# 1/rms applied as products leave PSUM, from parts of the unnormed h, at the memory attention's norm and both PEER norms

## The chip, the cores and the metric

The kernel runs on one core of one Trainium2 chip. The metric is the device time of one launch, in microseconds (us). Shown are the median of three runs and one profiled execution; the profile gives the span from the first to the last instruction beside the time of that execution.

## The reference

Two transformer blocks over 256 tokens of width 1024, in float32. Each block is a mixer and a mixture of experts (PEER); the first has attention to a memory between them. Every part starts with an RMS norm of the residual h. Cut to what matters here:

```python
def rms_norm(x, g):
    y = x * lax.rsqrt(jnp.mean(x * x, axis=-1, keepdims=True) + EPS)
    return y * g

def first_block(...):
    h = h + concat([o_gla, o_nsa]) @ w_out
    h = h + cross_attn(rms_norm(h, norm_xattn), rms_norm(mem, norm_mem), xa_wq, xa_wk, xa_wv, xa_wo)
    h = h + peer_ffn(rms_norm(h, norm_ffn), peer_wq, peer_subkeys, peer_down, peer_up)

def second_block(...):
    h = h + hybrid_mixer(rmsnorm(h, norm_mix_g), ...)      # ends in "@ w_out"
    h = h + peer_ffn_2(rmsnorm(h, norm_ffn_g), peer_w_q, peer_subkeys, peer_u, peer_v)

def peer_ffn(hn, wq, subkeys, down, up):
    q = hn @ wq                       # queries: 8 heads x 2 halves
    s = einsum(q, subkeys)            # then top 16 of each half, top 16 of the pairs, softmax
    act = gelu(einsum(hn, down[experts])) * gate    # uses hn once more
    return einsum(act, up[experts])
```

## The kernel before

**Layout.** h is kept with channels on the 128 partitions: eight chunks (KD = 8) of 128 channels by 256 tokens. A weight unit is 128x1024 float32 (512 KB): all that is needed for 128 output channels. Products are made from two rounded parts of each operand, a high and a low one, as three fp32r matmuls (`product`, L367 to L372): 8 chunks x 3 = 24 matmuls for a unit.

**Weight units.** `Split` (L317) fetches one: SyncE loads it into one of three ring slots (L334), ScalarE writes the high part into one of three part buffers (L338), VectorE the low part (L343; in the PEER layers' down phase GpSimd does it, L349). The ring slot is free when the low part is made, the part buffer when TensorE has used it. `submit` keeps two fetched units ahead of the one being multiplied; `flush(a, b)` fetches the next matrix's first two units while it works off the last two.

**Order.** There is no scheduler: the program is a list of steps, and each engine runs its part of every step in the order of that list, with semaphore waits. An instruction that waits holds everything that comes after it on its engine.

**Around the three norms.** `to_h` multiplies the eight units of `w_out`, `xa_wo` or `w_out_2`. Behind each product VectorE adds it to h (`AddToH`, L511), GpSimd squares the new chunk of h (L527), and TensorE adds the squares over the partitions with a matmul of ones into bank 7 (`SumSquares`, L549), one unit late; the last of them comes after all products. Then comes a `Barrier` (L618: each of four engines drains and waits for the others). `Normalize` (L554) follows: VectorE makes mean + eps (L571), ScalarE the root (L587, with a table load), VectorE the reciprocal (L573), and then for each chunk VectorE h x gain x 1/rms (L577), ScalarE the high part (L592), VectorE the low part (L581). The first product of the next matrix waits for these parts, chunk by chunk.

The next matrix is `xa_wq` (eight units), `peer_wq` (eight) or `peer_w_q_2` (sixteen). Each product leaves PSUM by a ScalarE copy (`Keep`, L495). After the last one TensorE makes the scores: L1523 in the memory attention, L1645 in the first PEER layer, L1649 in the second. Both PEER layers load their subkeys (L293) ahead of the third query unit, after the barrier.

In the text a *site* is one of these places: X (memory attention), P1, P2 (PEER layers). F(i) is the fetch of the site's unit i, high and low part.

## Time and profile before

| what | value |
|---|---|
| median of 3 runs | 2694.74 us (2690.89 to 2695.68) |
| the profiled execution's own time | 2693.68 us |
| its span | 2691.6 us |
| TensorE matmul busy | 2463.5 us, 92% of the span |
| VectorE / ScalarE / GpSimd busy | 1770.1 (66%) / 1173.3 (44%) / 769.5 us (29%) |
| mean granted TensorE clock | 0.949 |
| HBM read over the span | 142 GB/s |

A matmul's busy time overlaps the next one's, since they are pipelined: inside a run of products one starts every 0.12 us and is shown with 0.28 us. A row of the timeline that begins before an earlier row has ended is such an overlap. Idle time ahead of an instruction stands in brackets with what ended it.

### The profile page before, as it was taken

How to read it: one execution, taken by the hardware profiler on the slowest of the kernel's cores; microseconds unless marked ns; L12 is line 12 of the kernel's file. 1: busy time of each engine (PE TensorE's matmuls, PEld its weight loads, DVE VectorE, ACT ScalarE, POOL GpSimd, SP SyncE). 2: the span in 40 equal slices, each digit the busy share in tenths (PEclk: the TensorE clock that was granted, in tenths of full speed). 3: DMA queues.
4: the chain of work that ended last, by engine and by line, in shares of the span. 5: the costliest groups of instructions: out<-in, count | busy, mean ns of one | idle time of the engine just before them, and what ended most of it. 6: DMA issues, size and time to landing. Idle time of an engine off the chain costs nothing.

```text
span 2691.6 us, 38806 instructions
## 1 busy us (share of the span) xinstructions
PE 2463.5 (92%) x15906; PEld 2221.8 (83%) x15906; DVE 1770.1 (66%) x2770; ACT 1173.3 (44%) x1962; POOL 769.5 (29%) x366
## 2 busy tenths in 40 slices
PE   6978888999999999997878888789999999999997
PEld 5876788999999788886757877579999999888885
DVE  4564447978888555556577275465987888555554
ACT  3354334444444444443443344234444444444442
POOL 3000103886666000001000053201886666100000
PEclk8887899999999999998888989889999999999998
DMA  5421335555544666663422343145555445566663
GB/s 166 126 86 56 90 91 165 164 167 148 146 145 150 181 189 187 189 188 119 126 84 87 123 126 113 52 141 158 164 165 150 148 149 144 175 188 188 188 188 103
DMA packets 108566, 384.37 MB, mean 143 GB/s; under 512 B 13007, under 2 KB 16000, under 8 KB 107816
## 3 DMA queue, kind: packets, MB, share of 16 engines
q1 hardware_dynamic: 108392, 381.91, 47.3%
q8 instruction: 127, 2.08, 0.3%
q14 instruction: 47, 0.39, 0.0%
HBM read 380.79 MB, written 1.06 MB: 142 GB/s over the span
## 4 chain that ended last, share of the span: by engine, by line
PE 78%; DVE 13%; ACT 4%; POOL 2%; issue 1%; DMA 1%; SPq 0%; DVEq 0%; POOLq 0%; ACTq 0%
PE psum L370 21%; PE psum L371 21%; PE psum L372 21%; PE psum L1805 4%; POOL weight_parts L349 2%; PE psum L402 2%; PE psum L549 1%; PE psum L2425 1%; PE psum L2195 1%; DVE weight_parts L343 1%; DVE peer_experts L1713 1%; PE psum L1271 1%; ACT weight_parts L338 1%; DVE peer_experts L1689 1%; DVE peer_experts L1681 1%
## 5 line engine op out<-in xcount | busy, mean ns | idle before, releaser
L370 PE MATMUL psum<-acts_high,weight_parts 128*128 128x256 f32 x3152 | 933.8, 296 | 72.1 <-DVE acts_low L581 28.4
L371 PE MATMUL psum<-acts_low,weight_parts 128*128 128x256 f32 x3152 | 904.7, 287 | 0.0
L372 PE MATMUL psum<-acts_high,weight_parts 128*128 128x256 f32 x3152 | 904.4, 287 | 0.0
L349 POOL TENSOR_TENSOR weight_parts<-weight_ring,weight_parts 128x1024 fp32r<-128x1024 f32 x276 | 697.6, 2536 | 649.9 <-ACT weight_parts L338 649.2
L338 ACT ACTIVATE weight_parts<-weight_ring 128x1024 fp32r<-128x1024 f32 x681 | 714.8, 1050 | 184.1 <-PE psum L372 96.7
L343 DVE TENSOR_TENSOR weight_parts<-weight_ring,weight_parts 128x1024 fp32r<-128x1024 f32 x405 | 497.7, 1231 | 363.8 <-ACT weight_parts L338 363.7
L370 PEld LDWEIGHTS psum<-acts_high,weight_parts 128*128 128x128 f32 x3152 | 617.2, 196 | 90.0 <-issue 42.7
L371 PEld LDWEIGHTS psum<-acts_low,weight_parts 128*128 128x128 f32 x3152 | 618.7, 196 | 2.6 <-issue 1.7
L372 PEld LDWEIGHTS psum<-acts_high,weight_parts 128*128 128x128 f32 x3152 | 617.4, 196 | 0.0
L370 PE MATMUL psum<-weight_parts,peer_coef 128*128 128x512 f32 x1024 | 405.2, 396 | 4.0 <-issue 3.9
L372 PE MATMUL psum<-weight_parts,peer_coef 128*128 128x512 f32 x1024 | 405.0, 396 | 0.0
L371 PE MATMUL psum<-weight_parts,peer_coef 128*128 128x512 f32 x1024 | 405.0, 395 | 0.0
L1876 ACT ACTIVATE peer_coef<-peer_experts 128x256 fp32r<-128x256 f32 x256 | 106.6, 417 | 362.4 <-PE psum L372 361.3
L1789 DVE TENSOR_TENSOR peer_onehots<-peer_onehots,peer_gates 128x512 f32<-128x512 f32 x128 | 248.1, 1938 | 4.4
L370 PEld LDWEIGHTS psum<-weight_parts,peer_coef 128*128 128x128 f32 x1024 | 192.4, 188 | 51.3 <-issue 4.2
L372 PEld LDWEIGHTS psum<-weight_parts,peer_coef 128*128 128x128 f32 x1024 | 192.4, 188 | 46.6
L371 PEld LDWEIGHTS psum<-weight_parts,peer_coef 128*128 128x128 f32 x1024 | 192.4, 188 | 46.2
L527 POOL TENSOR_TENSOR peer_experts<-h 128x256 f32<-128x256 f32 x16 | 9.7, 614 | 745.0 <-DVE h L511 744.9
L1880 DVE TENSOR_TENSOR peer_coef<-peer_experts,peer_coef 128x256 fp32r<-128x256 f32 x256 | 108.9, 426 | 159.5 <-ACT peer_coef L1876 159.5
L1786 DVE TENSOR_TENSOR peer_onehots<-psum,peer_pairs 128x1024 f32<-128x1024 f32 x128 | 155.1, 1212 | 0.1
L1853 ACT ACTIVATE psum<-psum 128x4 f32<-128x4 f32 (+25 forms) x156 | 41.4, 266 | 248.5 <-PE psum L372 248.5
L527 POOL TENSOR_TENSOR work<-h 128x256 f32<-128x256 f32 x40 | 29.8, 759 | 412.2 <-DVE h L511 395.4
(388 smaller groups left out, 2508.0 us busy)
## 6 DMA issues: line engine op xcount, KB each, us to landing
weight_ring<-in_peer_down SPq DMA_DIRECT2D x128, 512.0 KB, 3.6
weight_ring<-in_peer_up SPq DMA_DIRECT2D x128, 512.0 KB, 3.6
weight_ring<-in_peer_u SPq DMA_DIRECT2D x128, 512.0 KB, 3.6
weight_ring<-in_peer_v SPq DMA_DIRECT2D x128, 512.0 KB, 4.2
weight_ring<-in_w_in SPq DMA_DIRECT2D x88, 512.0 KB, 3.7
weight_ring<-in_w_out SPq DMA_DIRECT2D x16, 512.0 KB, 3.6
weight_ring<-in_peer_w_q SPq DMA_DIRECT2D x16, 512.0 KB, 4.2
weight_ring<-in_w_in_v SPq DMA_DIRECT2D x10, 512.0 KB, 4.1
```

What stands on the lines that cost most here:

```text
L338: q.e.activation(self.high, self.ring, ACT.Copy).then_inc(*self.rounded.once())
L343: q.e.tensor_tensor(self.low, self.ring, self.high.bitcast(F32), ALU.subtract).then_inc(*self.unit.ready.once())
L349: q.e.tensor_tensor(self.low, self.ring, self.high.bitcast(F32), ALU.subtract).then_inc(*self.unit.ready.once())
L370: q.e.matmul(out, sh, mh, start=first, stop=False)
L371: q.e.matmul(out, sh, ml, start=False, stop=False)
L372: return q.e.matmul(out, sl, mh, start=False, stop=last)
L402: last = q.e.matmul(self.out, w[:, k, :], acts.whole[:, k, :], start=k == 0, stop=k == KD - 1)
L1786: q.e.tensor_tensor(self.hot, over(over(self.c.bank(7)[:, 0:P], GROUP, 1), 2, 1), over(x.pairs[:, :, tokens], P, 3), ALU.is_equal).then_in ...
L1789: q.e.tensor_tensor(self.hot[:, 0, :, :], self.hot[:, 0, :, :], over(x.gates[:, tokens], P, 2), ALU.mult).then_inc(*self.ready.once())
L1805: last = q.e.matmul(out, self.hot[:, 0, t, :], self.hot[:, 1, t, :], start=True, stop=True)
L1876: q.e.activation(self.high, self.src, ACT.Copy).then_inc(*self.rounded.once())
L1880: q.e.tensor_tensor(self.low, self.src, self.high.bitcast(F32), ALU.subtract).then_inc(*self.ready.once())
```

## The change

`to_h` also makes, right behind each `AddToH`, the two parts of h x gain of that chunk, without 1/rms (`GainedActs`), in a second pair of buffers (`acts_spare`). The next matrix is multiplied from these, and 1/rms, which is one number for a token, is multiplied in as each product leaves PSUM (`Late`, on VectorE in place of the ScalarE copy). 1/rms itself (`Rstd`) is made beside the products; the last `SumSquares` stands behind the second product. The PEER layers need the normed h for their down phase, so there eight steps `NormalizeChunk` stand between the query products: two behind each of the products 2 to 5 at P1, one behind each of 2 to 9 at P2. The barriers at the three sites go, and the subkeys' load waits for the last product of `to_h` in their place. `xn_reversed` lives in the spare buffers now. The norms of both mixers, of the memory and the final ones stay.

```diff
@@ -410,6 +410,48 @@
 
     def pool(self, q):
         self.evac.pool(q, self.out, self.done)
+
+class LateChannels(Channels):
+    phases = 2
+    def tensor(self, q):
+        super().tensor(q)
+        yield
+    def scalar(self, q):
+        yield
+        self.evac.scalar(q, self.out, self.done)
+    def vector(self, q):
+        yield
+        self.evac.vector(q, self.out, self.done)
+
+def late_channels(c, srcs, acts, evac, make_norm, beside=()):
+    beside, waiting = list(beside), []
+    def make(unit, n):
+        step = c.plan(LateChannels(c, unit, acts, evac(n)))
+        waiting.append(step)
+        if n == 1:
+            beside.extend(make_norm())
+        if n >= 1:
+            while waiting:
+                c.plan(waiting.pop(0))
+        if n >= 2:
+            for _ in range(-(-len(beside) // max(1, len(srcs) - 2 - n))):
+                c.plan(beside.pop(0))
+    for n, src in enumerate(srcs):
+        c.submit(src, lambda unit, n=n: make(unit, n))
 
 
 class Tokens:
@@ -495,6 +537,22 @@
         q.e.activation(self.dst, out, self.func, bias=0.0, scale=self.scale).then_inc(*self.kept.once())
 
 
+
+class Late(Evac):
+    def __init__(self, dst, scale, c):
+        self.dst, self.scale, self.c = dst, scale, c
+    def out_of_psum(self, c):
+        self.scaled = c.last_kept = c.mark("late_scaled")
+        return self.scaled
+    def vector(self, q, out, done):
+        q.wait_ge(done)
+        q.e.scalar_tensor_tensor(out=self.dst, in0=out, scalar=self.scale, in1=self.c.rms, op0=ALU.mult,
+                                 op1=ALU.mult).then_inc(*self.scaled.once())
 class AddToH(Evac):
 
 
@@ -549,6 +607,66 @@
         last = q.e.matmul(self.out, self.ones, self.squares, start=self.k == 0, stop=self.k == KD - 1)
         if self.summed:
             last.then_inc(*self.summed.once())
+
+class Rstd(Step):
+    def __init__(self, c, tmp):
+        self.tmp, self.sums, self.summed = tmp, c.bank(7)[:, 0:T], c.summed
+        self.mean, self.root, self.ready = c.mark("mean_square"), c.mark("root"), c.mark("rstd")
+        c.bank_free[7] = (self.mean,)
+        c.rms = tmp
+    def vector(self, q):
+        q.wait_ge(self.summed)
+        q.e.tensor_scalar(self.tmp, self.sums, 1.0 / D, EPS, ALU.mult, ALU.add).then_inc(*self.mean.once())
+        q.wait_ge(self.root)
+        q.e.reciprocal(self.tmp, self.tmp).then_inc(*self.ready.once())
+        q.wait_ge(self.ready)
+    def scalar(self, q):
+        q.wait_ge(self.mean)
+        q.e.activation(self.tmp, self.tmp, ACT.Sqrt).then_inc(*self.root.once())
+
+class NormalizeChunk(Step):
+    def __init__(self, c, x, gain, out, tmp, parts, k):
+        self.x, self.gain, self.out, self.tmp = x[:, k, :], gain[:, k:k + 1], out[:, k, :], tmp
+        self.high, self.low, self.parts_free = parts.high[:, k, :], parts.low[:, k, :], parts.free
+        self.normed, self.rounded, self.ready = c.mark("normed"), c.mark("acts_high"), c.mark("acts_low")
+        parts.marks[k] = self.ready
+    def vector(self, q):
+        q.e.scalar_tensor_tensor(out=self.out, in0=self.x, scalar=self.gain, in1=self.tmp, op0=ALU.mult,
+                                 op1=ALU.mult).then_inc(*self.normed.once())
+        q.wait_ge(self.rounded)
+        q.e.tensor_tensor(self.low, self.out, self.high.bitcast(F32), ALU.subtract).then_inc(*self.ready.once())
+    def scalar(self, q):
+        q.wait_ge(self.parts_free, self.normed)
+        q.e.activation(self.high, self.out, ACT.Copy).then_inc(*self.rounded.once())
+
+class GainedActs(Step):
+    def __init__(self, c, x, gain, parts, k, after=()):
+        self.x, self.gain, self.high, self.low = x, gain[:, k:k + 1], parts.high[:, k, :], parts.low[:, k, :]
+        self.after, self.parts_free = tuple(after), parts.free
+        self.rounded, self.ready = c.mark("acts_high"), c.mark("acts_low")
+        parts.marks[k] = self.ready
+    def scalar(self, q):
+        q.wait_ge(self.parts_free, *self.after)
+        q.e.activation(self.high, self.x, ACT.Identity, bias=0.0, scale=self.gain).then_inc(*self.rounded.once())
+    def vector(self, q):
+        q.wait_ge(self.rounded)
+        q.e.scalar_tensor_tensor(out=self.low, in0=self.x, scalar=self.gain, in1=self.high.bitcast(F32), op0=ALU.mult,
+                                 op1=ALU.subtract).then_inc(*self.ready.once())
 
 
 class Normalize(Step):
@@ -1363,7 +1481,7 @@
-        xr = Parts(*(c.sb(f"xn_reversed_{x}", [P, KD, T], ctx, F32R) for x in range(2)))
+        xr = Parts(spare.high, spare.low)
...
@@ -1475,25 +1593,29 @@
             c.flush(c.dram["w_out"][0], c.dram["w_out"][1])
             for k in range(4, KD):
                 c.plan(SplitActs(c, o[:, k, :], xn, k, [c.nsa_taken]))
-            to_h(c, c.dram["w_out"], xn, h, work)
-            c.flush(c.dram["xa_wq"][0], c.dram["xa_wq"][1])
-            c.barrier()
+            spare.free = memn.free
+            squares = to_h(c, c.dram["w_out"], xn, h, work, spare, c.gain("norm_xattn"),
+                           [c.dram["xa_wq"][0], c.dram["xa_wq"][1]])
             c.rotation = list(range(7))
-
-
-def to_h(c, srcs, acts, h, work):
+    return squares
+def to_h(c, srcs, acts, h, work, gained, gain, following):
 
     squares = Squares(work)
 
     def make(unit, n):
-        c.plan(Channels(c, unit, acts, AddToH(c, h, n, squares)))
+        evac = AddToH(c, h, n, squares)
+        c.plan(Channels(c, unit, acts, evac))
+        c.plan(GainedActs(c, h[:, n, :], gain, gained, n, [evac.added]))
         if n:
             c.plan(SumSquares(c, squares, n - 1))
 
     for n in range(KD):
         c.submit(srcs[n], lambda unit, n=n: make(unit, n))
-    c.flush()
-    c.plan(SumSquares(c, squares, KD - 1))
+    c.flush(*following)
+    return squares
 
 
 class AttendMemory(Step):
@@ -1592,7 +1714,7 @@
-def cross_attention(c, h, xn, work, tmp, mem_kv, following):
+def cross_attention(c, h, xn, work, tmp, mem_kv, spare, squares, following):
     k, v = mem_kv
     WIDTH = 3
     with ExitStack() as ctx:
@@ -1604,9 +1726,14 @@
         x.z = c.sb("xa_z", [P, WIDTH, 2], ctx)
         x.pt = c.sb("xa_pt", [P, XA_H, NT, T], ctx)
         x.area_free = [()] * WIDTH
-        c.plan(Normalize(c, h, c.gain("norm_xattn"), work, tmp[:, :], xn))
-        for n in range(KD):
-            c.channels(c.dram["xa_wq"][n], xn, Keep(x.q[:, n, :], scale=XA_DH ** -0.5))
+        def norm():
+            c.plan(SumSquares(c, squares, KD - 1))
+            c.plan(Rstd(c, tmp[:, :]))
+            return []
+        late_channels(c, [c.dram["xa_wq"][n] for n in range(KD)], spare,
+                      lambda n: Late(x.q[:, n, :], XA_DH ** -0.5, c), norm)
         c.flush(c.dram["xa_wo"][0], c.dram["xa_wo"][1])
         x.projected = [c.last_kept]
         for _ in pipeline(c, [lambda u, i=i, two=two: AttendMemory(c, x, i, two, u) for two in range(2)
@@ -1614,9 +1741,7 @@
             pass
         for n in range(KD):
             c.plan(MemoryValues(c, x, v, xn, n))
-        to_h(c, c.dram["xa_wo"], xn, h, work)
-        c.flush(*following)
-        c.barrier()
+        return to_h(c, c.dram["xa_wo"], xn, h, work, spare, c.gain("norm_ffn"), following)
 
 
 class Route(Step):
@@ -1949,7 +2074,7 @@
     pass
 
 
-def peer(c, h, xn, work, tmp, name, gain, half_dim, wq, subkeys, down, up, following=()):
+def peer(c, h, xn, work, tmp, gained, squares, name, gain, half_dim, wq, subkeys, down, up, following=()):
 
     n_q = 2 * PEER_H * half_dim // P
     with ExitStack() as ctx:
@@ -1961,10 +2086,14 @@
         area = x.experts[:, first_kept:NKEYS, :].rearrange("p a t -> p (a t)")
         sk = area[:, 0:n_q * P].rearrange("p (k n) -> p k n", k=n_q)
         qs = area[:, n_q * P:n_q * (P + T)].rearrange("p (k t) -> p k t", k=n_q)
-        c.plan(Normalize(c, h, gain, work, tmp[:, :], xn))
-        sk_came = c.load(sk, subkeys)
-        for n in range(n_q):
-            c.channels(wq[n], xn, Keep(qs[:, n, :]))
+        sk_came = c.load(sk, subkeys, after=[c.last_product])
+        def norm():
+            c.plan(SumSquares(c, squares, KD - 1))
+            c.plan(Rstd(c, tmp[:, :]))
+            return [NormalizeChunk(c, h, gain, work, tmp[:, :], xn, k) for k in range(KD)]
+        late_channels(c, [wq[n] for n in range(n_q)], gained, lambda n: Late(qs[:, n, :], 1.0, c), norm)
         c.flush(down[0], down[1])
         r = Routing(c, area[:, n_q * (P + T):], half_dim, qs, sk, [c.last_kept, sk_came], x.pairs, x.gates)
         routes = [Route(c, r, i) for i in range(NT)]
@@ -2730,9 +2859,9 @@
         merged = c.last_merged
         for k in range(KD):
             c.plan(SplitActs(c, ya[:, k, :], xn, k, [merged]))
-        to_h(c, c.dram["w_out_2"], xn, h, work)
-        c.flush(*following)
-        c.barrier()
+        gained = Parts(*(c.sb(f"acts_spare_2_{x}", [P, KD, T], ctx, F32R) for x in ("high", "low")))
+        squares = to_h(c, c.dram["w_out_2"], xn, h, work, gained, c.gain("norm_ffn_g_2"), following)
+    return gained, squares
 
 
 class Came(Step):
...
```

### The order of the instructions

VectorE at site X, before: the last additions to h, two low parts of `xa_wq`, then the norm, and all eight low weight parts behind it in a row.

```order
L511 TENSOR_TENSOR h<-h,psum 128x256 [waits multiplied] x3
L343 TENSOR_TENSOR weight_parts<-weight_ring,weight_parts 128x1024 [waits weights_high] x2
L571 TENSOR_SCALAR tmp<-psum 128x256 [waits pool_drained,vector_drained,squares_summed,scalar_drained,tensor_drained]
L573 RECIPROCAL tmp<-tmp 128x256 [waits root]
L577 SCALAR_TENSOR_TENSOR work<-h,gains,tmp 128x256 [waits rstd]
...
L343 TENSOR_TENSOR weight_parts<-weight_ring,weight_parts 128x1024 [waits weights_high] x8
```

VectorE at site X, changed (L668 is the low part of `GainedActs`, L623 and L625 are `Rstd`, L552 is `Late`):

```order
L569 TENSOR_TENSOR h<-h,psum 128x256 [waits multiplied]
L668 SCALAR_TENSOR_TENSOR acts_spare_low<-h,gains,acts_spare_high 128x256 [waits acts_high]
L343 TENSOR_TENSOR weight_parts<-weight_ring,weight_parts 128x1024 [waits weights_high] x2
L623 TENSOR_SCALAR tmp<-psum 128x256 [waits squares_summed]
L625 RECIPROCAL tmp<-tmp 128x256 [waits root]
L552 SCALAR_TENSOR_TENSOR xa_q<-psum,tmp 128x256 [waits multiplied,rstd]
L552 SCALAR_TENSOR_TENSOR xa_q<-psum,tmp 128x256 [waits multiplied]
L343 TENSOR_TENSOR weight_parts<-weight_ring,weight_parts 128x1024 [waits weights_high]
L552 SCALAR_TENSOR_TENSOR xa_q<-psum,tmp 128x256 [waits multiplied]
```

The two low parts ahead of L623 are those of units 2 and 3; unit 4's now stands behind the reciprocal and two `Late` steps.

VectorE at P1, before: nothing but weight parts behind the norm (the COPY puts the iota row into bank 7).

```order
L581 TENSOR_TENSOR acts_low<-work,acts_high 128x256 [waits acts_high] x2
L343 TENSOR_TENSOR weight_parts<-weight_ring,weight_parts 128x1024 [waits weights_high] x8
L1771 COPY psum<-iota 128x128 [waits mean_square]
```

VectorE at P1, changed, behind the third query product (L643 and L646 are `NormalizeChunk`):

```order
L343 TENSOR_TENSOR weight_parts<-weight_ring,weight_parts 128x1024 [waits weights_high]
L552 SCALAR_TENSOR_TENSOR peer_experts<-psum,tmp 128x256 [waits multiplied]
L643 SCALAR_TENSOR_TENSOR work<-h,gains,tmp 128x256
L646 TENSOR_TENSOR acts_low<-work,acts_high 128x256 [waits acts_high]
L643 SCALAR_TENSOR_TENSOR work<-h,gains,tmp 128x256
L646 TENSOR_TENSOR acts_low<-work,acts_high 128x256 [waits acts_high]
L343 TENSOR_TENSOR weight_parts<-weight_ring,weight_parts 128x1024 [waits weights_high]
```

Four such rounds follow one another. At P2 a round has one L643 and one L646, and there are eight rounds. On ScalarE the high part of a chunk (L650) stands ahead of the next unit's high weight part (L338) in the same way.

SyncE at P1, before and changed: the place of the subkeys' load stays, its wait differs.

```order
L334 DMA weight_ring<-in_peer_wq 128x1024 [waits weights_low_by_vector] x2
L293 DMA peer_experts<-in_peer_subkeys 128x1024 [waits pool_drained,vector_drained,loaded_6,scalar_drained,tensor_drained]
L334 DMA weight_ring<-in_peer_wq 128x1024 [waits weights_low_by_vector] x6
```

```order
L334 DMA weight_ring<-in_peer_wq 128x1024 [waits weights_low_by_vector] x2
L293 DMA peer_experts<-in_peer_subkeys 128x1024 [waits loaded_6,multiplied]
L334 DMA weight_ring<-in_peer_wq 128x1024 [waits weights_low_by_vector] x6
```

The six units behind it still can't be fetched before the subkeys' load has been issued.

## Rows read from the trace of the kernel before

**Rows 1.** The page's part 4: the chain that ended last, by engine.

```profile
PE 78%; DVE 13%; ACT 4%; POOL 2%; issue 1%; DMA 1%; SPq 0%; DVEq 0%; POOLq 0%; ACTq 0%
```

**Rows 2.** Timeline, TensorE at site X: start, duration, engine, line, operands, idle before.

```profile
316.23 0.60 PE L549 MATMUL psum<-work,ones 128*128 128x256 f32 x2
...
325.53 0.55 PE L370 MATMUL psum<-acts_high,weight_parts 128*128 128x256 f32 x1 [6.32 <-DVE acts_low L581]
...
331.11 0.28 PE L370 MATMUL psum<-acts_high,weight_parts 128*128 128x256 f32 x1
...
351.90 1.35 PE L1523 MATMUL psum<-mem_k,xa_q 128*128 128x256 f32 x5 [0.47 <-ACT xa_q L495]
```

**Rows 3.** Timeline, VectorE at site X.

```profile
316.43 0.42 DVE L511 TENSOR_TENSOR h<-h,psum 128x256 f32<-128x256 f32 x1 [2.88 <-PE psum L372]
...
319.88 0.42 DVE L571 TENSOR_SCALAR tmp<-psum 128x256 f32<-128x256 f32 x1 [0.34 <-DVEq L630]
322.14 1.75 DVE L573 RECIPROCAL tmp<-tmp 128x256 f32<-128x256 f32 x1 [1.84 <-ACT tmp L587]
323.93 0.88 DVE L577 SCALAR_TENSOR_TENSOR work<-h,gains,tmp 128x256 f32<-128x256 f32 x2
324.96 0.43 DVE L581 TENSOR_TENSOR acts_low<-work,acts_high 128x256 fp32r<-128x256 f32 x1
325.30 0.48 DVE L577 SCALAR_TENSOR_TENSOR work<-h,gains,tmp 128x256 f32<-128x256 f32 x1
...
330.87 1.23 DVE L343 TENSOR_TENSOR weight_parts<-weight_ring,weight_parts 128x1024 fp32r<-128x1024 f32 x1 [0.52 <-ACT weight_parts L338]
```

**Rows 4.** Timeline, ScalarE at site X.

```profile
324.51 0.75 ACT L592 ACTIVATE acts_high<-work 128x256 fp32r<-128x256 f32 x2 [2.40 <-DVE work L577]
...
329.47 0.42 ACT L592 ACTIVATE acts_high<-work 128x256 fp32r<-128x256 f32 x1 [0.31 <-DVE work L577]
329.80 1.04 ACT L338 ACTIVATE weight_parts<-weight_ring 128x1024 fp32r<-128x1024 f32 x1
...
351.47 0.38 ACT L495 ACTIVATE xa_q<-psum 128x256 f32<-128x256 f32 x1 [1.55 <-PE psum L372]
```

**Rows 5.** Windows: us, PE, PEld, DVE, ACT, POOL busy, granted clock, DMA share, GB/s.

```profile
324.00:330.00 6.00, 4.47 (x19) 4.41 (x20) 5.71 (x16) 3.36 (x9) 0.00 (x0) 0.50 0.01 3
```

**Rows 6.** Timeline, VectorE and TensorE: both ends of sites P1 and P2.

```profile
401.87 0.42 DVE L511 TENSOR_TENSOR h<-h,psum 128x256 f32<-128x256 f32 x1 [2.88 <-PE psum L372]
...
437.27 2.06 PE L1645 MATMUL psum<-peer_experts 64*128 64x128 f32 x32 [0.47 <-ACT peer_experts L495]
...
1804.74 0.42 DVE L511 TENSOR_TENSOR h<-h,psum 128x256 f32<-128x256 f32 x1 [2.88 <-PE psum L372]
...
1863.19 3.84 PE L1649 MATMUL psum<-peer_experts 128*128 128x128 f32 x32 [0.47 <-ACT peer_experts L495]
```

**Rows 7.** By form: min/median/max ns, first and last start.

```profile
L2547 DVE SCALAR_TENSOR_TENSOR hy_x<-psum,gains,hy_x x16: 482/483/484, 1556.4 to 1658.5; 128x255 f32<-128x255 f32 x16
...
L577 DVE SCALAR_TENSOR_TENSOR h<-h,gains,tmp x8: 479/829/834, 1253.0 to 1257.6; 128x256 f32<-128x256 f32 x8
```

**Rows 8.** SyncE timeline, then DMA issues of single loads at P1 and P2 (us to landing).

```profile
406.01 0.43 SPq L334 DMA_DIRECT2D weight_ring<-in_peer_wq  x1
...
weight_ring<-in_peer_wq SPq DMA_DIRECT2D x1, 512.0 KB, 4.3
...
weight_ring<-in_peer_wq SPq DMA_DIRECT2D x1, 512.0 KB, 5.2
...
weight_ring<-in_peer_w_q SPq DMA_DIRECT2D x1, 512.0 KB, 5.8
...
weight_ring<-in_peer_w_q SPq DMA_DIRECT2D x1, 512.0 KB, 6.6
```

**Rows 9.** Windows in the first mixer, columns as in rows 5.

```profile
60.00:65.00 5.00, 2.93 (x25) 2.72 (x23) 4.96 (x7) 0.83 (x2) 5.00 (x6) 1.00 0.68 213
65.00:70.00 5.00, 2.24 (x17) 2.05 (x19) 4.99 (x9) 1.85 (x3) 1.07 (x2) 0.80 0.00 0
```

17 lines of the change are left out of this document (11 added, 6 removed).

## The prediction

> **What bounds the kernel.** I read the page first: of the chain that ended last, 78% is TensorE's own work and 13% VectorE's [rows 1]. So most of the span is TensorE's products, which the change leaves as they are, and what it can give lies in the places where TensorE waits. The timeline of TensorE around the three norms shows such a place. At X the last sum of squares but one starts at 316.23, the next product only at 325.53 after 6.32 us of idle time put down to the low parts of the activations, the second unit at 331.11 and the first score at 351.90 [rows 2]. VectorE's timeline shows the wait as one chain: last addition to h at 316.43, mean at 319.88, reciprocal at 322.14, first normed chunk at 323.93, first low part at 324.96 [rows 3]. The first unit then takes 5.6 us (325.53 to 331.11) where the six behind it take 2.88 each. The window 324 to 330 shows why: the granted clock there is 0.50, so 1.2 GHz, after an idle stretch [rows 5]. I measure each site from the start of the last addition to h to the start of the first score: 35.47 us at X (316.43 to 351.90), 35.40 at P1 (401.87 to 437.27), 58.45 at P2 (1804.74 to 1863.19) [rows 2, 3, 6]. The work ahead of and behind these stretches is the same in both kernels, and the stretches follow one another through the data, so what they lose the program loses.
>
> **Prices.** A product's result can be taken 3.08 us after its first matmul (351.47 against 331.11 + 6 x 2.88) [rows 2, 4], and the next unit follows after 2.88. A sum of squares between two units adds 0.42. Reading the chain [rows 3, 4]: mean to reciprocal 2.26 (table load and root lie between), reciprocal to the next VectorE instruction 1.79; a scalar_tensor_tensor lets the next one start after 0.40, a high weight part on ScalarE (329.80) lets the low one start 1.07 later (330.87), that one lets VectorE go on after 1.15 and TensorE after 1.37. A chunk's norm: high part 0.58 behind its start, low part 1.03, next instruction 1.37; ScalarE can go on 0.33 after the high part.
>
> No row shows a scalar_tensor_tensor with the product in PSUM and 1/rms in SBUF. The nearest, L2547, has the product in PSUM and takes 0.48; the worst row of that instruction is 0.83 (L577 in place on h) and the best 0.48 [rows 7]. I take 0.48, by L2547, and keep 0.83. That L2547 takes as long from PSUM as L577 does from SBUF [rows 3, 7] speaks against a rule. The Trainium skill, VectorE: DVE Perf Modes, in its part on the TRN2 errata, gives VectorE 62 cycles more for a PSUM source than for an SBUF source, 65 ns, and says that ScalarE sits closer to PSUM. By that rule some 18 of these evictions on the path would cost 1.2 us more; the rows don't show it.
>
> **Site X.** Removed from the path: the norm's chain. Added beside `to_h`: eight scaled high parts on ScalarE and eight low parts on VectorE, 0.4 to 0.5 us each in a round of 3.30 us in which VectorE has 1.65 of work and ScalarE 1.05; nothing. The last chunk's low part comes at about 316.43 + 0.5 + 0.45 + 0.5 = 317.9. The first product may start right after the sum of squares, and needs chunk 7 only at 319.2: hidden, with 1.3 us to spare. So result 0 is there at 316.43 + 3.30 = 319.73, result 1 at 322.61. The last sum of squares, from 322.4 to 323.0, moves onto the path: 0.42. Behind it: mean 323.1, reciprocal 325.36, two late evictions at 327.15 and 327.55, and only then unit 4's low part (327.95), since it is queued behind them. TensorE gets unit 4 at 329.32; it would have liked it at 328.59. The new wait costs 0.73. From there on TensorE sets the pace: result 7 at 329.32 + 3 x 2.88 + 3.08 = 341.04, eviction 0.48, score 0.05 later: 341.6. Before 351.90: **10.3 us won**.
>
> **Site P1.** Same start, first results at 405.17 and 408.05. Two things differ. The subkeys' load waits for the last product and holds the units 2 to 4 behind it in SyncE's queue: issue at 401.95, then 0.43 each, and the burst lands as before, 4.3 and 5.2 us after issue [rows 8]: unit 2 at 406.7, unit 3 at 408.0. High 0.05 later, low 1.07, TensorE 1.37: unit 2 at 409.17, 1.1 late. Unit 3's low part (409.13) holds the mean to 410.3; reciprocal 412.56, evictions 414.35 and 414.75, unit 4's low part 415.15, TensorE 416.52 (1.6 late). Then come four rounds, each on VectorE: eviction 0.40, one chunk 1.37, the second chunk up to its high part 0.58, ScalarE to the next weight part 0.33, its low part 1.07 later, 1.15: **4.90 us where TensorE needs 2.88**. Low parts of units 5, 6, 7 and of the next matrix's first at 420.05, 424.95, 429.85, 434.75; then eviction 6 (435.90), a low part (436.30), eviction 7 (437.45), score 437.98. Before 437.27: **0.7 us lost**. All that the early start wins is given back, as the norm that the down phase needs moves to where it delays weight parts.
>
> **Site P2.** Results 0 and 1 at 1808.04 and 1810.92. The subkeys are 1 MB here; units 2 and 3 land 5.8 and 6.6 us after issues at 1805.25 and 1805.68 [rows 8]: 1811.05 and 1812.28. Unit 2 starts at 1813.54 (2.6 late); mean 1814.55, reciprocal 1816.80, unit 4's low part 1819.40, TensorE 1820.77. Eight rounds with one chunk: 0.40 + 0.58 + 0.33 + 1.07 + 1.15 = 3.53 against 2.88. Low part of unit 5 at 1822.93, of unit 12 seven rounds later at 1847.64, TensorE 1849.01; unit 15 8.64 later, result 3.08, eviction 0.53: 1861.3. Before 1863.19: **1.9 us won**.
>
> Removed barriers: at X the mean started 0.34 after VectorE's last work [rows 3], all inside the chain already counted. The 24 copies that leave ScalarE give nothing; it is idle most of these stretches.
>
> **Sum.** -10.3 + 0.7 - 1.9 = -11.5 us. The profiled execution took 2693.68, so 2682.2; the median of the runs lies 1.06 above it: **2683.2 us**. About 0.2% (5.4 us) is what a measurement can tell from no change.
>
> **Rivals.**
> *Half clock in parts of the PEER stages.* In P1's rounds TensorE works 3.1 of 4.9 us. In the first mixer, 60 to 65, it is busy 2.93 of 5 and still granted 1.00; at 2.24 of 5 it is 0.80 [rows 9]. [...] At 1.2 GHz a product takes about 5.1 us, 0.2 over a round; but the scores (2.06 us at P1) and the first down product would start slow, 2 us each at most: 2685 to 2687, still faster.
> *Half clock that stays, slower than before.* If it held through P2 from unit 2 on, 14 products of 5.14, 72 us, stood in place of 47: +25, P1 +4, and with -11.5 the sum is +17.5: 2712. It turns the sign with 11.5 us lost and decides (0.2% slower) with 17, eleven products that each take 1.6 more than a round of 3.53 covers. For it: the waits of 2.6 and 1.6 us at the start. Against: at X the clock was back by 331 after five us of products [rows 2, 5]. The Trainium skill, TensorE: Matmul & The Clock Gate, Part 1, says that the half rate is the default and that activity releases it, which is the rule by which such a fall could last.
> *Dear evictions and chunk norms.* If the new instructions take 0.83: the rounds grow by 1.05 and 0.70, with the ends 5.6 us at P1, 6.3 at P2, 1.1 at X, 13.0 in all: 2696, no change. The 0.83 rows stand beside GpSimd's squares at 1253; GpSimd has nothing to do in these stretches, so it is unlikely.
> *The norm still gates.* If 1/rms came in time for less delay (loads landing sooner, 3.6 us as single loads do), P1 and P2 would win 1 and 2 us more: 2680.
>
> **How the numbers follow.** Forecast 0.70, loads sooner 0.06, part half clock 0.13, dear instructions 0.07, staying half clock 0.04. The forecast's own error: 0.6 us for each handover that I read 0.05 wrong in twelve rounds, 2 us for the median of the runs. From the sooner loads to part half clock with these errors: 2679.5 to 2689.5, which leaves out the last two cases and some tails. Faster by over 0.2%: 0.89, the first three cases; within 0.2% 0.07, the dear instructions; slower 0.04.
>
> **What would show it.** In the changed profile TensorE's 6.3 us waits for the activations' low parts are gone at three sites and the clock at X stays 1.0. X is some 25 us long with one wait of about 0.7 ahead of unit 4, put down to L343; P1 is about 36 us with waits near 2 us ahead of units 5, 6 and 7, P2 about 56.5 with waits of 0.65. L552 and L643 take 0.48, and L338 starts 0.33 after L650. The prediction is wrong if P1 is clearly shorter than 35.4 (then VectorE's queue is not the limit I take it for), if X wins under 9, or if the products show 0.41 in place of 0.28 us there.

## The result, and the profile after

The changed kernel took **2672.38 us** (median of 4 runs, 2670.28 to 2679.52), the kernel before 2692.81 us beside it (2690.31 to 2695.68): a ratio of 0.9928, with a 95% interval of 0.9906 to 0.9951. That is 20.4 us faster, where 11.5 were forecast. The direction was right and the size was not: the median lies 7 us below the lower end of the range. The profiled execution was the slowest of the four, 2679.52 us with a span of 2677.7, 14.2 us under the profiled one of before.

The chain that ended last is still TensorE's for the most part (compare [rows 1]):

```profile
PE 76%; DVE 14%; ACT 4%; POOL 2%; DMA 2%; issue 1%; SPq 0%; POOLq 0%; DVEq 0%; ACTq 0%
```

**Site X.** TensorE's timeline in the changed kernel, to be held against [rows 2]:

```profile
312.59 0.60 PE L607 MATMUL psum<-work,ones 128*128 128x256 f32 x2
...
318.63 0.59 PE L607 MATMUL psum<-work,ones 128*128 128x256 f32 x2
...
336.55 1.78 PE L1645 MATMUL psum<-mem_k,xa_q 128*128 128x256 f32 x7 [0.52 <-DVE xa_q L552]
```

No wait stands between the last sum of squares and the evictions ahead of the scores (0.52 us); the 6.32 us are gone. VectorE's timeline (compare [rows 3]):

```profile
312.79 0.42 DVE L569 TENSOR_TENSOR h<-h,psum 128x256 f32<-128x256 f32 x1
313.79 0.48 DVE L668 SCALAR_TENSOR_TENSOR acts_spare_low<-h,gains,acts_spare_high 128x256 fp32r<-128x256 f32 x1 [0.58 <-ACT acts_spare_high L664]
...
319.26 0.42 DVE L623 TENSOR_SCALAR tmp<-psum 128x256 f32<-128x256 f32 x1 [0.86 <-PE psum L607]
320.17 1.75 DVE L625 RECIPROCAL tmp<-tmp 128x256 f32<-128x256 f32 x1 [0.48 <-ACT tmp L630]
321.96 0.76 DVE L552 SCALAR_TENSOR_TENSOR xa_q<-psum,tmp 128x256 f32<-128x256 f32 x2
```

and ScalarE's (compare [rows 4]):

```profile
316.09 1.06 ACT L338 ACTIVATE weight_parts<-weight_ring 128x1024 fp32r<-128x1024 f32 x1 [1.39 <-PE psum L372]
317.17 1.28 ACT L630 ACT_TABLE_LOAD   x1
319.72 0.42 ACT L630 ACTIVATE tmp<-tmp 128x256 f32<-128x256 f32 x1 [1.27 <-DVE tmp L623]
```

The table load now starts at 317.17, two microseconds ahead of the mean that the root waits for, and mean to reciprocal takes 0.91 us (319.26 to 320.17) where it took 2.26. The window 324 to 330, at 0.50 before [rows 5], has the full clock:

```profile
324.00:330.00 6.00, 6.00 (x54) 6.00 (x53) 4.48 (x6) 2.12 (x2) 0.00 (x0) 1.00 0.64 222
```

Site X is 336.55 - 312.79 = 23.76 us long, 11.7 less than before; 25.15 were forecast.

**Site P1.** VectorE's timeline shows the round with two chunks that was forecast:

```profile
403.22 0.42 DVE L552 SCALAR_TENSOR_TENSOR peer_experts<-psum,tmp 128x256 f32<-128x256 f32 x1
403.56 0.48 DVE L643 SCALAR_TENSOR_TENSOR work<-h,gains,tmp 128x256 f32<-128x256 f32 x1
404.52 0.42 DVE L646 TENSOR_TENSOR acts_low<-work,acts_high 128x256 fp32r<-128x256 f32 x1 [0.48 <-ACT acts_high L650]
404.86 0.48 DVE L643 SCALAR_TENSOR_TENSOR work<-h,gains,tmp 128x256 f32<-128x256 f32 x1
405.82 0.42 DVE L646 TENSOR_TENSOR acts_low<-work,acts_high 128x256 fp32r<-128x256 f32 x1 [0.48 <-ACT acts_high L650]
406.77 1.23 DVE L343 TENSOR_TENSOR weight_parts<-weight_ring,weight_parts 128x1024 fp32r<-128x1024 f32 x1 [0.52 <-ACT weight_parts L338]
407.92 0.42 DVE L552 SCALAR_TENSOR_TENSOR peer_experts<-psum,tmp 128x256 f32<-128x256 f32 x1
```

From eviction to eviction it is 407.92 - 403.22 = 4.70 us, and three times in it VectorE stands still for ScalarE (0.48, 0.48, 0.52). TensorE pays for it ahead of units 5, 6 and 7, and then ahead of the scores, where it waits for two low parts of the next matrix's weights and two evictions:

```profile
408.05 0.39 PE L370 MATMUL psum<-acts_spare_high,weight_parts 128*128 128x256 f32 x1 [1.59 <-DVE weight_parts L343]
412.75 0.38 PE L370 MATMUL psum<-acts_spare_high,weight_parts 128*128 128x256 f32 x1 [1.60 <-DVE weight_parts L343]
417.44 0.39 PE L370 MATMUL psum<-acts_spare_high,weight_parts 128*128 128x256 f32 x1 [1.63 <-DVE weight_parts L343]
423.93 3.79 PE L1770 MATMUL psum<-peer_experts 64*128 64x128 f32 x32 [3.39 <-DVE peer_experts L552]
```

The scores took 3.79 us where they took 2.06 [rows 6]. The windows (columns as in [rows 5]) show why:

```profile
415.00:420.00 5.00, 3.37 (x28) 3.17 (x28) 3.30 (x7) 2.09 (x5) 0.00 (x0) 1.00 0.42 127
420.00:424.00 4.00, 0.61 (x7) 0.40 (x5) 3.48 (x6) 1.76 (x2) 0.00 (x0) 0.89 0.34 85
424.00:428.00 4.00, 4.00 (x33) 3.78 (x34) 0.08 (x1) 0.24 (x1) 0.00 (x0) 0.50 0.57 208
428.00:432.00 4.00, 4.00 (x28) 4.00 (x28) 2.20 (x12) 3.97 (x5) 1.27 (x1) 0.75 0.01 2
```

In the rounds, at 3.4 of 5 us busy, the clock stays at 1.00 (2.4 GHz); TensorE then stands idle for 3.39 us, and the scores and the first down product run at 0.50 (1.2 GHz). P1 is 423.93 - 388.78 = 35.15 us long (before 35.40, forecast 36.1); P2 is 1849.36 - 1794.40 = 54.96 (before 58.45, forecast 56.5).

### The profile page after: what moved, and what is told of

Its sections match the earlier page's. It is cut to its first block, busy times and chain, and to the rows that moved or that the text cites. A ratio compares the mean times of both kernels' runs of the same rounds, so it can differ in the third digit from the quotient of the medians.

```text
span 2677.7 us, 38829 instructions
## 1 busy us (share of the span) xinstructions
PE 2459.3 (92%) x15906; PEld 2214.3 (83%) x15906; DVE 1783.9 (67%) x2810; ACT 1169.1 (44%) x1946; POOL 765.3 (29%) x366
## 4 chain that ended last, share of the span: by engine, by line
PE 76%; DVE 14%; ACT 4%; POOL 2%; DMA 2%; issue 1%; SPq 0%; POOLq 0%; DVEq 0%; ACTq 0%
PE psum L370 21%; PE psum L371 20%; PE psum L372 20%; PE psum L1930 4%; POOL weight_parts L349 2%; PE psum L402 2%; PE psum L607 1%; DVE weight_parts L343 1%; PE psum L2554 1%; ACT weight_parts L338 1%; PE psum L2324 1%; DVE peer_experts L1838 1%; PE psum L1389 1%; DVE peer_experts L1837 1%; DVE peer_experts L1814 1%
## 5 line engine op out<-in xcount | busy, mean ns | idle before, releaser
L370 PE MATMUL psum<-acts_high,weight_parts 128*128 128x256 f32 x2896 | 856.3, 296 | 52.1 <-DVE weight_parts L343 20.7
L371 PE MATMUL psum<-acts_low,weight_parts 128*128 128x256 f32 x2896 | 828.7, 286 | 0.0
L372 PE MATMUL psum<-acts_high,weight_parts 128*128 128x256 f32 x2896 | 828.1, 286 | 0.0
L338 ACT ACTIVATE weight_parts<-weight_ring 128x1024 fp32r<-128x1024 f32 x681 | 714.5, 1050 | 163.2 <-PE psum L372 64.7
L370 PEld LDWEIGHTS psum<-acts_high,weight_parts 128*128 128x128 f32 x2896 | 564.8, 195 | 68.4 <-issue 22.9
L371 PEld LDWEIGHTS psum<-acts_low,weight_parts 128*128 128x128 f32 x2896 | 566.0, 195 | 2.7 <-issue 1.7
L372 PEld LDWEIGHTS psum<-acts_high,weight_parts 128*128 128x128 f32 x2896 | 564.7, 195 | 0.0
L1980 ACT ACTIVATE peer_experts<-psum 128x256 f32<-128x256 f32 (+32 forms) x250 | 79.3, 317 | 152.1 <-PE psum L372 152.0
```

Of the source, the lines that this page charges most:

```text
L338: q.e.activation(self.high, self.ring, ACT.Copy).then_inc(*self.rounded.once())
L370: q.e.matmul(out, sh, mh, start=first, stop=False)
L371: q.e.matmul(out, sh, ml, start=False, stop=False)
L372: return q.e.matmul(out, sl, mh, start=False, stop=last)
L1980: last = q.e.activation(self.x.experts[:, self.n, n:T], out[:, n:T], ACT.Gelu_apprx_tanh)
```

## The experiments

I cut each profiled execution at the same events: the last addition to h ahead of a site and the first score of that site. The table holds all of them, in us, from the timelines (to 0.1). "First mixer" is the start of the last addition ahead of X; "attention" runs from X's first score to the last addition ahead of P1; "PEER 1" from P1's first score to that layer's last addition; "mixer 2" to the last addition ahead of P2; "PEER 2" from P2's first score to the last addition of all. The first four rows have every product behind the norm; the second four are executions of the changed kernel.

| kernel | first mixer | X | attention | P1 | PEER 1 | mixer 2 | P2 | PEER 2 |
|---|---|---|---|---|---|---|---|---|
| before | 316.4 | 35.5 | 50.0 | 35.4 | 809.7 | 557.8 | 58.5 | 814.8 |
| placement | 316.8 | 35.5 | 50.0 | 35.4 | 809.7 | 557.8 | 58.4 | 814.9 |
| split_early | 313.4 | 33.9 | 50.0 | 33.8 | 810.9 | 558.1 | 56.8 | 816.3 |
| no_barriers | 317.8 | 33.8 | 50.8 | 34.1 | 811.7 | 556.3 | 56.5 | 812.3 |
| changed | 312.8 | 23.8 | 52.2 | 35.1 | 814.0 | 556.5 | 55.0 | 814.7 |
| same_again | 314.2 | 23.8 | 52.2 | 34.0 | 814.9 | 556.9 | 54.7 | 814.7 |
| after_c | 312.8 | 23.8 | 50.0 | 33.5 | 812.8 | 556.6 | 54.8 | 810.7 |
| after_d | 315.9 | 23.8 | 50.8 | 35.2 | 813.8 | 556.6 | 54.8 | 810.7 |
| x_only | 314.1 | 23.8 | 52.2 | 34.4 | 809.7 | 558.0 | 56.8 | 812.9 |
| peers_only | 313.5 | 33.9 | 50.0 | 33.6 | 811.3 | 557.8 | 55.5 | 814.8 |
| no_chunks | 317.0 | 23.8 | 50.8 | 25.0 | 810.5 | 553.1 | 50.6 | 812.7 |
| pipelined | 311.1 | 23.8 | 48.3 | 26.6 | 809.7 | 558.0 | 50.0 | 813.3 |
| pipelined_sk | 311.5 | 23.8 | 52.2 | 24.6 | 809.7 | 557.6 | 46.2 | 813.3 |

My first theory was that the stages add up as forecast, with a few prices misread (theory A); against it stood that the buffers' place gives part of the gain, and that the profiled execution was not typical.

### same_again, x_only, peers_only, placement

`same_again` is the changed kernel unaltered. `x_only` and `peers_only` keep the late scaling at one kind of site:

```diff
-        late_channels(c, [wq[n] for n in range(n_q)], gained, lambda n: Late(qs[:, n, :], 1.0, c), norm)
+        if late:
+            late_channels(c, [wq[n] for n in range(n_q)], gained, lambda n: Late(qs[:, n, :], 1.0, c), norm)
+        else:
+            for n in range(n_q):
+                c.channels(wq[n], xn, Keep(qs[:, n, :]))
```

with `Normalize` ahead and the barrier back at those sites, and the same at X. `placement` is the kernel before with one pair of buffers moved:

```diff
-        xr = Parts(*(c.sb(f"xn_reversed_{x}", [P, KD, T], ctx, F32R) for x in range(2)))
+        xr = Parts(spare.high, spare.low)
```

> The changed kernel once more, unaltered, to see which parts of its difference recur. Theory A (the stages): 11.7 us fewer from the last addition ahead of X to its first score, 0.2 us fewer at P1, 3.4 at P2 recur within 0.3 us each; median near 2672. Theory B (chance of the run): the 3.6 us by which the first mixer was already shorter at 312.79, and the 4.3 us that PEER 1 lost behind its scores, do not recur; then they differ by over 1 us here and the profiled span lies nearer 2669 than 2678.

> The late scaling at X alone; P1 and P2 have the norm ahead of the products again, with their barriers. Theory A: X wins 11.7 us, P1 and P2 are as in the kernel before, and if the first mixer's 3.6 us belong to X's side (its reversed buffers lie in the spare ones) they show too: 2.3 us are given back in the attention by a lower clock, so 2692.8 - 11.7 - 3.6 + 2.3 = 2679.8. Rival B: the 3.6 us were chance, 2683.4. Rival C: the PEER sites give much more than the profile showed, then this kernel stays at 2686 or above.

> The late scaling at P1 and P2 alone; X as before. Theory A by the two profiles: P1 -0.2, P2 -3.4, PEER 1 behind its scores +4.3, in sum +0.7: 2693.5, and 2689.9 if the first mixer's 3.6 us come from where its reversed buffers lie. Rival: the loss behind P1's scores was chance of the profiled run, then 2689.2, or 2685.6 with the first mixer's 3.6 us.

> The kernel before, with the one pair of buffers moved: the reversed activations of the first mixer lie in a spare pair allocated ahead of the others, as in the changed kernel; no norm is changed. If the 3.6 us by which the first mixer was shorter come from the place of the buffers (products with 0.1167 in place of 0.120 us each): 2689.2, with the last addition ahead of X near 312.8. If not: within 1 us of 2692.8, and that addition near 316.4.

| kernel | median us | runs | ratio to before | 95% |
|---|---|---|---|---|
| before | 2692.57 | 23 | | |
| same_again | 2672.27 | 6 | 0.9921 | 0.9904 to 0.9937 |
| x_only | 2677.68 | 6 | 0.9936 | 0.9917 to 0.9954 |
| peers_only | 2687.07 | 12 | 0.9976 | 0.9966 to 0.9986 |
| placement | 2690.38 | 12 | 0.9992 | 0.9982 to 1.0002 |

So the 20 us recur; x_only has about 15 of them and peers_only about 5. These are not the worth of the late scaling at those sites alone: both versions also keep the changed order of the weight splits at the sites that are not late, and those got shorter too. By the table the three sites together give 14.3 us in x_only (11.7 + 1.0 + 1.6) and 6.4 in peers_only (1.6 + 1.8 + 3.0). The move of the buffers gives nothing that can be told: its sites are those of before to 0.1 us. The first mixer's 3.6 us are not shown to be a part of the change: in the eight executions with the changed kernel's code up to X it ends between 311.1 and 317.0 (mean 313.7), in the five with the norm ahead of X between 313.4 and 317.8 (315.6). Whether the 1.9 us between the means are more than chance is open. The half clock falls on different stretches there from one execution to the next. Windows of placement, then of same_again, over the same products:

```profile
200.00:205.00 5.00, 5.00 (x27) 4.78 (x27) 3.72 (x20) 1.02 (x2) 0.00 (x0) 0.51 0.71 190
```

```profile
200.00:205.00 5.00, 5.00 (x43) 4.70 (x42) 3.71 (x20) 1.93 (x6) 0.00 (x0) 1.00 0.66 181
```

27 matmuls against 43 in five busy microseconds.

I had not expected that the sites that were *not* late would be shorter. The versions differ from the kernel before there in one respect, the place of `flush(*following)`. So the next batch took the change's side effects one by one.

### split_early and no_barriers

`split_early` moves only the split of the next two units' weights, ahead of the last additions:

```diff
-    c.flush()
+    c.flush(*following)
     c.plan(SumSquares(c, squares, KD - 1))
```

`no_barriers` only drops three lines:

```diff
-            c.barrier()
```

> The kernel before with one thing moved: the weights of the two units behind each of the three norms are split ahead of the last additions to h, as the changed kernel does too, so VectorE has no low part (2.77 us for two) between the last addition and the mean; no product is scaled late. In x_only and peers_only the sites with the norm still in front were shorter by this: X 33.9 for 35.5, P1 34.4 for 35.4, P2 56.8 for 58.5. Theory: the same here, -1.6 - 1.0 - 1.7 = -4.3, so 2688.3. Rival: those gains came from the other changes, then 2692.6, with 35.5, 35.4 and 58.5 us.

> The kernel before without the three barriers ahead of the norms at X, P1 and P2; nothing else moved. In the changed kernel ScalarE's table load for the root ran at 317.17, ahead of the mean at 319.26, and mean to reciprocal took 0.91 us in place of 2.26. Theory: the barrier held the load, so without it each site is 1.3 us shorter: 34.2, 34.1 and 57.2 us, and the time 2692.6 - 4 = 2688.6. Rival (the load waits for the mean anyway, and the changed order of ScalarE's other work let it run early): 35.5, 35.4 and 58.5 us, within 1 us of 2692.6.

split_early: 2688.85 us (12 runs) against 2690.75 (17 runs), ratio 0.9994 (0.9982 to 1.0007). no_barriers: 2687.72 (12) against 2688.96 (17), ratio 0.9990 (0.9979 to 1.0002). Neither can be told from no change by its time, so the gain forecast for the whole is not shown; the sites do show it, 1.6 us each in split_early (35.5 to 33.9, 35.4 to 33.8, 58.5 to 56.8) and 1.7, 1.3 and 2.0 in no_barriers. Other stretches ran longer in their profiles (PEER 1 by 1.2 and 2.0). A part of such a difference is where the half clock falls: P1 in x_only has the order of split_early, but gave 1.0 and not 1.6, and 11.0 to 13.5 us behind its last addition its granted clock was 0.50, where split_early had 1.00. In split_early no low part stands between the addition and the mean (2.00 us, before 3.45):

```profile
313.39 0.42 DVE L511 TENSOR_TENSOR h<-h,psum 128x256 f32<-128x256 f32 x1 [0.92 <-PE psum L372]
315.39 0.42 DVE L571 TENSOR_SCALAR tmp<-psum 128x256 f32<-128x256 f32 x1 [1.58 <-PEq L622]
317.66 1.75 DVE L573 RECIPROCAL tmp<-tmp 128x256 f32<-128x256 f32 x1 [1.84 <-ACT tmp L587]
```

In no_barriers the mean starts 3.03 us behind the last addition (317.77), 0.42 earlier than before, and the table load has run ahead. Its ScalarE and VectorE:

```profile
315.61 1.28 ACT L587 ACT_TABLE_LOAD   x1
...
320.80 0.41 DVE L571 TENSOR_SCALAR tmp<-psum 128x256 f32<-128x256 f32 x1
321.25 0.42 ACT L587 ACTIVATE tmp<-tmp 128x256 f32<-128x256 f32 x1 [4.35 <-DVE tmp L571]
321.69 1.75 DVE L573 RECIPROCAL tmp<-tmp 128x256 f32<-128x256 f32 x1 [0.48 <-ACT tmp L587]
```

0.89 us from mean to reciprocal, as in the changed kernel, with nothing but the barriers taken out. So it was the barrier that held the table load: the load waits for what ScalarE's queue waits for, and that was the barrier, not the mean. The Trainium skill, ScalarE: Activation LUTs, What ACT_TABLE_LOAD costs, gives 1283 ns for a load and a drain of 1380 ns with it. The load agrees with the rows (1.28); of the drain they show nothing, since in [rows 3] the mean starts at 319.88 and the reciprocal 2.26 us later with load and root between. By the page's two figures the change would have saved an estimated 2.7 us between mean and reciprocal; it saved 1.35.

### no_chunks, pipelined and pipelined_sk

These ask what sets P1's and P2's rounds. `no_chunks` returns `[]` from `norm()` in `peer`, for both PEER layers, and so leaves out the normed activations that the down products need. `pipelined` does the same work in another order:

```diff
 class NormalizeChunk(Step):
+    phases = 2
...
                                  op1=ALU.mult).then_inc(*self.normed.once())
+        yield
         q.wait_ge(self.rounded)
...
     def scalar(self, q):
+        yield
         q.wait_ge(self.parts_free, self.normed)
...
     def make(unit, n):
+        while halfway:
+            c.plan(halfway.pop(0))
...
-                c.plan(beside.pop(0))
+                halfway.append(c.plan(beside.pop(0)))
```

`pipelined_sk` also plans the subkeys' load in `norm()`, that is behind the loads of the query units 2 and 3, with the same mark to wait for.

> The changed kernel without the chunks of the norm at P1 and P2: it leaves out the normed activations that both layers' down products take (they take what is left of earlier ones). An upper bound for what the chunks' place costs. Theory (the chunks on VectorE set the rounds): P1 near 28 us and P2 near 51, scores at full clock, 2672.3 - 7 - 4 - 4 = 2657, and pipelined within 2 us of it. Rival (loads or clock set the pace): P1 stays above 33, 2670.

> The changed kernel; of each chunk of the norm VectorE does the product first and the low part only after the next weights' low part, and ScalarE rounds the chunk behind the next weights' high part. No work is added or left out. Theory (VectorE's round of 4.69 us at P1 is half waiting for ScalarE, 0.5 us per chunk and 0.5 ahead of the weights' low part): the round falls to 0.34 + 2 x 0.40 + 1.2 + 2 x 0.36 = 3.1 at P1, P1 to 29 us, P2 to 52, and with TensorE busy again the scores run at full clock, so PEER 1 behind them gets its 4.3 us back: 2672.3 - 6 - 3 - 4 = 2659. Rival A (the loads set the pace): waits of about 1.5 us stay ahead of units 4 to 7 at P1, 2671. Rival B (the half clock comes from the waits ahead of units 2 to 4, not from the rounds): P1 and P2 win 9, the scores stay slow, 2663.

> As pipelined, and the subkeys are loaded after the query weights of units 2 and 3 at P1 and P2, not ahead of them. Theory (the subkeys' transfer held unit 2 for 1.1 us at P1 and 2.6 at P2): 1 us more at P1 and 2 at P2, 3 below pipelined. Rival: the loads of units 2 and 3 wait for their ring slots, not for the subkeys, or the burst only moves on to unit 4: within 1 us of pipelined.

| kernel | median us | runs | ratio to before (2690.75, 17 runs) | 95% |
|---|---|---|---|---|
| no_chunks | 2659.33 | 5 | 0.9890 | 0.9871 to 0.9908 |
| pipelined | 2659.46 | 5 | 0.9890 | 0.9872 to 0.9908 |
| pipelined_sk | 2654.26 | 5 | 0.9868 | 0.9848 to 0.9889 |

Doing the chunks without waiting for ScalarE is worth as much as not doing them. VectorE's timeline of pipelined:

```profile
399.08 0.41 DVE L554 SCALAR_TENSOR_TENSOR peer_experts<-psum,tmp 128x256 f32<-128x256 f32 x1
399.41 0.87 DVE L646 SCALAR_TENSOR_TENSOR work<-h,gains,tmp 128x256 f32<-128x256 f32 x2
400.20 1.21 DVE L343 TENSOR_TENSOR weight_parts<-weight_ring,weight_parts 128x1024 fp32r<-128x1024 f32 x1
401.34 0.75 DVE L650 TENSOR_TENSOR acts_low<-work,acts_high 128x256 fp32r<-128x256 f32 x2
402.01 0.41 DVE L554 SCALAR_TENSOR_TENSOR peer_experts<-psum,tmp 128x256 f32<-128x256 f32 x1
```

The round is 402.01 - 399.08 = 2.93 us, with no idle time in it, for 4.70: what was taken away is the three waits and the chunk that stood ahead of the weights' high part on ScalarE. P1 falls from 33.5 to 35.2 us in the four executions of the changed kernel to 26.6, and P2 from 54.8 to 50.0. Then the scores and the window on them:

```profile
409.80 2.06 PE L1775 MATMUL psum<-peer_experts 64*128 64x128 f32 x32 [2.05 <-DVE peer_experts L554]
```

```profile
405.00:410.00 5.00, 2.95 (x26) 2.75 (x26) 4.95 (x11) 1.88 (x3) 0.00 (x0) 1.00 0.68 187
410.00:414.00 4.00, 4.00 (x50) 3.88 (x49) 0.05 (x1) 2.09 (x3) 0.00 (x0) 1.00 0.56 167
```

The scores wait 2.05 us instead of 3.4 and run at full clock, and PEER 1 takes its 809.7 us again. Rival A falls, since the rounds have no wait left. Rival B falls too: the wait ahead of unit 2 is 0.90 us here and the scores are fast, and it is 0.65 in after_c below, with no other ahead of unit 5, and they are slow. The median met the forecast of 2659, but not by its terms: the sites gave more than forecast (7.8 and 4.9 us on the mean, for 6 and 3), and of the 4 us taken for PEER 1 only 1.7 belong to the scores (see after_c and after_d). Beside the kernel before that ran with each, the step from the changed kernel to pipelined is 11.0 us (20.3 to 31.3), from median to median 12.8.

With pipelined_sk P1 is 2.0 us shorter still and P2 3.8. The expectation puts 1 and 2 us down to the subkeys' transfer. SyncE's timeline shows a longer hold. Of the changed kernel, then of pipelined_sk:

```profile
388.78 0.33 SPq L293 DMA_DIRECT2D peer_experts<-in_peer_subkeys  x1
389.15 1.38 SPq L334 DMA_DIRECT2D weight_ring<-in_peer_wq  x3
```

```profile
380.76 3.63 SPq L334 DMA_DIRECT2D weight_ring<-in_peer_wq  x2
387.45 0.33 SPq L293 DMA_DIRECT2D peer_experts<-in_peer_subkeys  x1
387.82 5.61 SPq L334 DMA_DIRECT2D weight_ring<-in_peer_wq  x3
```

The subkeys wait for the last product of `to_h`, and the query weights stood behind that wait in SyncE's queue with their ring slots long free. Ahead of it, units 2 and 3 are issued 6.7 and 3.4 us before the last addition to h (387.46), where the changed kernel issues them 0.4 and 0.9 after it (388.78), with slots that came free at 382.06 and 385.36 (ends of the low parts that had used them). VectorE's idle time for unit 2 (4.56 us at P1 in the changed kernel) is gone, and the mean starts 6.47 us behind the last addition at both sites, for 8.49 and 10.94 in pipelined. The prediction had named this queue; the size it gave it, 1.1 us at P1 and 2.6 at P2, was that of TensorE's first wait. How much of the 2.0 and 3.8 us is the hold and how much the transfer ahead of the units is not separated. This version is the best of the study: 36.5 us faster than the kernel before.

### after_c and after_d

Both are the changed kernel again, for their profiles. What they are to decide is why the stages add up to less than the medians show.

> The changed kernel a third time, for its profile alone. Both profiled executions so far were among its slowest (2679.5 and 2680.8, granted clock 0.953 and 0.952, where the median is 2672.3 at 0.955) and both had the attention at a clock of 0.54 to 0.78 (52.2 us for 50.0) and P1's scores at half clock (PEER 1 in 814.0 and 814.8 us for 809.7). Theory (where the half clock falls is the chance of each execution, and the 6 us between the stages' sum and the medians are executions without these two losses): an execution near 2672 shows at least one of the two stretches at full clock. Rival (the two losses are in every execution): 52.2 and 814 again, and a fast execution is fast in the first mixer.

> As after_c, once more. Theory: time and mean granted clock go together, 2.7 us for each 0.001, as in the runs so far (2680.8 at 0.952, 2674.2 at 0.955, 2667.4 at 0.957).

after_c took 2670.21 us (mean granted clock 0.956), after_d 2676.95 (0.951). after_c has the attention at 50.0 us, where two executions had 52.3 and 52.2: one window of each, changed kernel first, then after_c:

```profile
350.00:355.00 5.00, 2.27 (x7) 1.70 (x8) 0.86 (x3) 1.62 (x5) 0.00 (x0) 0.65 0.01 3
```

```profile
350.00:355.00 5.00, 3.54 (x13) 2.86 (x14) 1.12 (x2) 1.00 (x3) 0.00 (x0) 0.81 0.01 3
```

But P1's scores were slow in all four executions (3.79, 3.51, 2.63 and 3.78 us, each behind an idle stretch of 3.4), and PEER 1 took 812.8 to 814.9. So the attention's loss is chance and the scores' is not, which neither theory had.

The scores are only a part of what PEER 1 lost, 3.1 to 5.2 us. The high parts of its weights (L338) stand in the four executions 2.2, 1.5, 1.1 and 2.1 us behind those of before, counted from the first score, once the stretch behind the scores is over (from 195 us on): that is the price of the slow scores, 1.7 on the mean. In same_again another 1.6 us are lost some 440 us behind the scores, where split_early loses 1.6 as well, and in all four 2.0 in the last 12 us of the stage. Windows on the last products of PEER 1, of before, the changed kernel and no_barriers:

```profile
1241.00:1249.00 8.00, 6.07 (x28) 4.00 (x28) 2.53 (x7) 0.00 (x0) 4.33 (x8) 1.00 0.00 0
1228.00:1236.00 8.00, 6.81 (x21) 4.62 (x22) 3.17 (x8) 0.00 (x0) 3.03 (x5) 0.57 0.01 2
1238.00:1246.00 8.00, 6.51 (x20) 4.51 (x20) 3.28 (x7) 0.00 (x0) 2.83 (x5) 0.57 0.01 2
```

These last 2.0 us are not the scores' doing: no_barriers has them with scores at full clock (2.06 us), and peers_only, with slow scores, has not. Why all four executions of the changed kernel have them is open.

after_d shows one more such stretch, at P2, where no rounds went before: TensorE was busy in all of 1796 to 1801, then waited 3.55 us for unit 2, and ran at half clock behind it.

```profile
1806.09 0.38 PE L370 MATMUL psum<-acts_spare_high,weight_parts 128*128 128x256 f32 x1 [3.55 <-DVE weight_parts L343]
1806.00:1811.00 5.00, 4.91 (x28) 4.91 (x29) 4.46 (x7) 2.68 (x4) 0.00 (x0) 0.66 0.56 207
```

P2 took 54.8 us even so; in the other three the same wait was 2.1 to 2.2 us, and the clock stayed full.

The expected 2.7 us for each 0.001 of the clock did not hold for after_d: 0.951 would give some 2683 by it. The Trainium skill, TensorE: Matmul & The Clock Gate, Part 1, says that the gate's phase at the start differs from run to run, so that the same kernel shows different numbers of slow matmuls. The table agrees: the first mixer alone spans 312.8 to 315.9 in four executions of one kernel.

## Why the prediction was wrong in size, step by step

Two steps failed: the 2.26 us from mean to reciprocal, with VectorE's rounds put too long beside it, which together with TensorE's pace make 5 us at the sites, and the assumption that nothing outside the sites moves, where 4 us were lost and some 8 won, the latter without a known cause.

- **Where the time is lost and won** was right. The waits for low parts at X are gone, X holds most of the gain (11.7 of the 16.3 us that the sites give), P1 gives next to nothing for the reason named (the norm of the down phase in VectorE's queue: 25.0 us without it), and P2 stands between. The sign "P1 clearly shorter than 35.4" was to mean that this queue is not the limit; after_c had P1 at 33.5 with the same rounds, so the sign was too sharp for the scatter of the loads.
- **X, -10.3 forecast, -11.7 measured.** Failed step: "mean 323.1, reciprocal 325.36", the 2.26 us. I read the table load as part of the chain from mean to root [rows 3] and wrote that the removed barriers were "all inside the chain already counted". no_barriers shows that the barrier placed the load there: 0.89 us. With the load went the 0.73 us wait ahead of unit 4, and that is all that the 1.35 us were worth on TensorE's path. The rest is TensorE's pace: a unit took 2.80 us with the new activations' buffers where 2.88 was taken from before; why is open.
- **P1, +0.7 forecast.** The four executions have 35.1, 34.0, 33.5 and 35.2, on the mean 34.5, -0.9. The round was put at 4.90 and is 4.69 in all four: an eviction gives VectorE back after 0.33 and not 0.40, and a chunk after 1.30 and not 1.37, twice. That makes 0.8 in four rounds. TensorE got a unit 1.28 us behind the start of its low part (406.77 to 408.05), where 1.37 was taken. The other 1.35 of the table load is here too, but in the profiled execution it was eaten by a late load: the mean starts 9.95 us behind the last addition, where 8.43 was forecast; in after_c it is 8.32, and P1 33.5.
- **P2, -1.9 forecast, -3.6 measured** on the mean. Rounds of 3.38 us for 3.53, eight times, give 1.2 and the table load 1.35; against them the mean starts 11.15 us behind the last addition (1805.55) where 9.81 was forecast. The rest is TensorE's pace in the units behind the rounds.
- **The rival "half clock in parts of the PEER stages"** was true of P1 and came on top of the forecast. I gave it 0.13, and priced the scores and the first down product at up to 2 us each; they cost 1.1 to 2.2 us together. What I had not seen is what comes before the fall. In the rounds, at 3.4 of 5 us, the clock stayed full, so it did not come where I expected it; it comes after them, where TensorE waits 3.4 us for two low parts and two evictions. At P2 the last chunk is done 14 us ahead of the scores, the last wait is 0.52, and the scores took as long as before (3.84 us); there the half clock came in after_d alone, behind a wait of 3.55 for unit 2. PEER 1 as a whole took 4.2 us more on the mean of the four (813.9 against 809.7), of which 1.7 belong to this rival.
- **Dear evictions**: no. The late product out of PSUM takes less than the 0.48 that I took from L2547. By form in the changed kernel:

```profile
L552 DVE SCALAR_TENSOR_TENSOR peer_experts<-psum,tmp x24: 415/418/426, 401.4 to 1848.9; 128x256 f32<-128x256 f32 x24
...
L643 DVE SCALAR_TENSOR_TENSOR work<-h,gains,tmp x16: 473/476/481, 403.6 to 1834.1; 128x256 f32<-128x256 f32 x16
```

  The two forms differ in where the product or h comes from and in the scalar, a constant in L552 and a column of gains in L643. The third form, L2547 of [rows 7], tells them apart: from PSUM with a column of gains, 483 ns. So PSUM for SBUF makes 7 ns (483 against 476) and the column for the constant 65 (483 against 418). The Trainium skill, VectorE: DVE Perf Modes, in its part on the TRN2 errata, has 65 ns more for PSUM than for SBUF; these rows speak against it.
- **Staying half clock, slower than before**: did not come.
- **The rest of the program, put at nothing.** "What they lose the program loses" took every stretch outside the sites as unchanged. In the mean of the four executions PEER 1 is 4.2 us longer (1.7 behind the scores, the rest later), the attention 1.3 longer, the first mixer 2.5, mixer 2 1.1 and PEER 2 2.1 shorter.
- **The sum.** With these means: sites -11.7 - 0.9 - 3.6 = -16.3 (forecast -11.5), PEER 1 +4.2, the other stretches -4.4. In all -16.5 in the spans, and the times are 2676.9 on the mean against the 2693.68 of before, -16.8. The medians say -20.4. The 3.6 us between are executions: the four profiled ones were 4.5 above the median of all twelve (2672.4), the one of before 0.9 above its own. So 5 of the 9 us by which I missed are prices of the sites, 4 went the other way in PEER 1, and about 8 lie outside both: 4.4 net in stretches that the change does not touch, and the 3.6 between profiled and median executions. The cause of these 8 is open. The kernel before itself moved by as much as half of them, with medians of 2692.8, 2692.6, 2690.8 and 2689.0 beside the four sets of runs; after_c and after_d are 18.8 and 12.0 us below the last of these. In x_only and peers_only the medians (-14.9 and -5.5) are within 1 us of what the sites give (14.3 and 6.4), so they show no lasting effect outside the sites.

## What to carry to other kernels

When work is moved off a chain into the queue of an engine that also feeds the bottleneck, count how often that engine waits *inside* the moved work: here the product, round and subtract of a chunk cost 1.30 us of VectorE's queue for 0.75 of work, and putting other work between the product and the subtraction won 11 to 13 us where the move itself had won 20. Look at what stands behind each wait in a DMA queue: one early load with a late condition held two loads whose ring slots had been free for 7 and 4 us. And a barrier can cost more than its own wait: it held a table load that could have run under the last products.

## What the runs showed of the hardware

- A table load runs as soon as ScalarE's queue reaches it, ahead of the wait of the instruction that needs it (317.17 with its input at 319.26; 315.61 in no_barriers); behind a barrier it stands on the path with 1.28 us.
- Of the stretches behind the last additions in the late versions, TensorE's clock fell to half behind each idle stretch of 3.39 to 4.12 us, five ahead of P1's scores and two ahead of P2's unit 2 (after_d and peers_only), the last two with TensorE fully busy before. It stayed full behind each of 2.05 to 2.30 us (P1's scores in pipelined, P2's unit 2 in five executions).
- A VectorE scalar_tensor_tensor of 128x256 took 483 ns from PSUM and 476 from SBUF with a column as its scalar, and 418 from PSUM with a constant.
- The scatter of this kernel goes mostly with the granted clock: the changed kernel's six runs in same_again go from 2667.41 us at 0.957 to 2680.82 at 0.952. after_d, 2676.95 at 0.951, lies off that line.
